# The first pair's down products directly behind its up products, the sort of all tokens after them

## The reference

```python
hid = jax.nn.silu(xi @ w1[e]) * (xi @ w3[e])
yb  = hid @ w2[e]                      # for the tokens that chose expert e
y   = y.at[buf_tok].add(yb * gate)     # two experts per token
```

## Time and profile before

| | |
|---|---|
| median of 3 runs | 2505.44 us |
| the profiled execution | 2509.44 us |
| its span | 2507.4 us |
| TensorE's matmuls busy | 2052.0 us (82%) |
| VectorE busy | 628.4 us (25%) |
| ScalarE busy | 417.3 us (17%) |
| DMA | 769.97 MB, mean 307 GB/s |

### The profile page before, as it was taken

The page is one execution under the profiler, slowest core; times in us unless marked ns, Lnnn a source line. Parts: engine busy times, 40 slices in busy tenths (PEclk is TensorE's granted clock), DMA queues, the critical chain, the costliest instruction groups (busy, mean ns, idle before and its releaser), DMA issues.

```text
span 2507.4 us, 29820 instructions
## 1 busy us (share of the span) xinstructions
PE 2052.0 (82%) x12400; PEld 1221.0 (49%) x12401; DVE 628.4 (25%) x1382; ACT 417.3 (17%) x780; POOL 0.2 (0%) x4
## 2 busy tenths in 40 slices
PE   7999996666667999756666799999877899999776
PEld 4775742222223684222222378885323678873333
DVE  2553330000012224000000244324211542244112
ACT  3141120000001212000000024212101233112111
POOL 0000000000000000000000000000000000000000
PEclk8999999999999999999999999999999999999999
DMA  9338759999999425999999942225999642257996
GB/s 402 126 142 374 319 232 426 426 426 426 426 426 427 171 93 219 425 426 426 426 426 426 425 182 106 97 107 224 426 425 426 258 164 101 101 202 294 425 426 279
DMA packets 66925, 769.97 MB, mean 307 GB/s; under 512 B 7424, under 2 KB 7936, under 8 KB 8448
## 3 DMA queue, kind: packets, MB, share of 16 engines
q1 hardware_dynamic: 66528, 768.19, 73.9%
q10 hardware_dynamic: 288, 0.26, 0.0%
HBM read 767.38 MB, written 1.05 MB: 306 GB/s over the span
## 4 chain that ended last, share of the span: by engine, by line
PE 53%; DMA 43%; DVE 2%; ACT 1%; issue 1%; SPq 0%; ACTq 0%; DVEq 0%
DMA slab<-in_triples 42%; PE psum L437 14%; PE psum L469 13%; PE psum L2107 5%; PE psum L734 5%; PE psum L2136 2%; PE psum L2032 2%; PE psum L540 2%; PE psum L2046 1%; DMA slab<-in_dense 1%; PE psum L2075 1%; PE psum L1284 1%; PE psum L2056 1%; PE psum L787 1%; DVE slab L677 0%
## 5 line engine op out<-in xcount | busy, mean ns | idle before, releaser
L2107 PE MATMUL psum<-slab 128*32 128x512 f32 (+1 forms) x3840 | 476.1, 599 | 329.4 <-DMA slab<-in_triples 327.4
L2107 PEld LDWEIGHTS psum<-slab 128*32 128x32 f32 x3840 | 160.6, 109 | 643.6 <-DMA slab<-in_triples 457.1
L437 PE MATMUL psum<-slab 128*128 128x256 f32 (+5 forms) x1464 | 372.2, 412 | 5.6 <-DVE slab L1885 3.8
L469 PE MATMUL psum<-slab 128*128 128x256 f32 x1504 | 340.2, 387 | 5.2 <-ACT slab L2345 2.3
L469 PEld LDWEIGHTS psum<-slab 128*128 128x128 f32 x1504 | 290.8, 194 | 53.1 <-issue 9.7
L437 PEld LDWEIGHTS psum<-slab 128*128 128x128 f32 (+2 forms) x1464 | 262.2, 190 | 107.6 <-issue 68.6
L2136 PE MATMUL psum<-slab 128*32 128x512 f32 (+1 forms) x1920 | 229.9, 604 | 52.4 <-DMA slab<-in_triples 52.4
L2191 DVE TENSOR_TENSOR slab<-psum,slab 128x512 f32<-128x512 f32 (+1 forms) x44 | 24.5, 558 | 783.5 <-PE psum L2107 546.0
L2032 PE MATMUL psum<-slab 128*128 128x256 f32 x704 | 171.5, 385 | 1.2 <-DVE slab L2195 1.2
L2032 PEld LDWEIGHTS psum<-slab 128*128 128x128 f32 x704 | 125.9, 189 | 52.0 <-issue 36.0
L2136 PEld LDWEIGHTS psum<-slab 128*32 128x32 f32 x1920 | 52.7, 110 | 177.6 <-issue 94.6
(11 more groups left out here) (461 smaller groups left out, 1453.7 us busy)
## 6 DMA issues: line engine op xcount, KB each, us to landing
slab<-in_triples SPq DMA_DIRECT2D x360, 1536.0 KB, 27.4
slab<-in_dense SPq DMA_DIRECT2D x73, 2048.0 KB, 10.3
slab<-in_pairs SPq DMA_DIRECT2D x18, 2048.0 KB, 8.4
slab<-in_dense SPq DMA_DIRECT2D x2, 1680.0 KB, 21.6
slab<-in_vec SPq DMA_DIRECT2D x1, 2589.5 KB, 32.9
slab<-in_dense SPq DMA_DIRECT2D x1, 1328.0 KB, 27.5
slab<-in_dense SPq DMA_DIRECT2D x2, 640.0 KB, 17.9
slab<-in_xT SPq DMA_DIRECT2D x1, 1024.0 KB, 8.7
```

The source lines that it names most:

```text
L437: ins = mm(out_ap, lhs, rhs, start=(n == 0), stop=(n == len(pairs) - 1), skip_group_check=True)
L469: ins = mm(psum[:, b, S * j:S * j + S], narrow(s, width)[:, k, c0 + P * j:c0 + P * j + P], src[:, k, :], start=(k == 0), stop=(k == KD - 1 ...
L2107: ins = mm(psum[WIN * g:WIN * g + WIN, n, :], xg[:, k, WIN * g:WIN * g + WIN], weights_of(w, j, g, extra), start=(k == 0), stop=(k == KD - ...
```

## The change

The sort moves behind the pair's down products, on all three engines. TensorE waits for both evictions of the down products before it, since the sort writes the same two banks; the first triple doesn't wait for them again. ScalarE's copies of the first triple's windows come after its part of the sort instead of before the eviction of the down products; VectorE turns the gates and evicts its half before its part of the sort.

```diff
@@ pe_pair
                 ins.then_inc(sems["unit_done"], 1)
-            pe_sort(q)
             fc = 4 if kind == 1 else 2
             pe_turn_hidden(q, fc)
...
                 ins.then_inc(sems["unit_done"], 1)
+            q.e.wait_ge(sems["half_ready"], q.due("half_ready"))
+            q.e.wait_ge(sems["results_ready"], q.due("results_ready"))
+            pe_sort(q)
@@ pe_triple
-            q.e.wait_ge(sems["half_ready"], q.due("half_ready"))
-            q.e.wait_ge(sems["results_ready"], q.due("results_ready"))
+            if not begin:
+                q.e.wait_ge(sems["half_ready"], q.due("half_ready"))
+                q.e.wait_ge(sems["results_ready"], q.due("results_ready"))
             pe_scatter(q, 0, KD // 2, begin)
@@ act_pass
-            if sort is not None:
-                act_sort(q, sort)
             q.e.wait_ge(sems["hid_turned"], q.due("hid_turned"))
             A.activation(hidT[:, 0:f // P, :], banks(0, 1, f // P, P), ACT.Copy).then_inc(sems["hidT_ready"], 1)
-            if ahead is not None:
+            if ahead is not None and sort is None:
                 act_windows(q, ahead)
             q.e.wait_ge(sems["unit_done"], q.due("unit_done", down))
             A.activation(ysl[:, 0:512], psum[:, 2, :], ACT.Copy).then_inc(sems["half_ready"], 1)
             q.skip("unit_done", 1 if pair or kind == 2 else 2)
+            if sort is not None:
+                act_sort(q, sort)
+                act_windows(q, ahead)
@@ dve_pair
             V.tensor_tensor(gated, gated, along(gates[:, :, 0:2], CAP), ALU.mult).then_inc(sems["gated_ready"], 1)
+            dve_gates_turned(q)
+            dve_results(q, 2)
             dve_sort(q, sort)
             dve_windows_copied(q, 0)
-            dve_gates_turned(q)
-            dve_results(q, 2)
```

## The result

The changed kernel took 2510.82 us, the median of 20 runs, against 2507.28 us for the kernel before, also of 20. The ratio is 1.0017 with a 95% interval of 1.0010 to 1.0023, so it is slower by 2.5 to 5.8 us. Measured again beside other kernels it was 1.0011 (1.0002 to 1.002). The forecast was 5.5 us slower, and 2510.9 us in time. That the time fits to 0.1 us is luck: the forecast started from 2505.4 us, the median of three runs, which is 1.8 us under the median of twenty, and its figure for the change is too high by about as much (5.5 us against 3.5 between the medians). The profiled execution has a span of 2509.2 us.

The account below looks back on a forecast made before the run. The stream of weight parts was taken to set each expert stage's time. At full clock 3.5 us faster, half clock 9.0 slower: net 5.5 slower, 2505.4 + 5.5 = 2510.9 us, range 2501.5 to 2518.

Parts of the forecast that it names:

- The chain of TensorE: Pair to first triple: new waits start the triple 3.9 us later in kind 1 (six slots), 6.45 in kind 2 (three).
- The stream at full clock: Weight parts per stage: gains of 2.8 and 2.5 us in kind 1, losses of 0.9 each in kind 2; 3.5 faster.
- Not removed but moved to the sort's other side: Kind 1 stream: the standstill from about 355 to 363 us would come from about 366 to 373 instead.
- The clock: TensorE's new gaps bring half clock: 1.3 us per kind 1 stage, 3.2 per kind 2 stage, 9.0 slower in all.
- A: TensorE's new gaps: no half clock follows them, so 3.5 us faster, 2501.9; chance 0.22.
- B: All four stages: half clock from before the first triple's first unit, 10.3 to 16 us slower, 2516 to 2521; chance 0.20.
- C: All stages: TensorE's lateness counts in full, 20.7 us, 2526; chance 0.03.
- D: Behind the sort: windows within 1 us and clock held, 2 us per stage more gained, 2494; chance 0.03.

Follow-up runs that it names:

- kernel with filled gaps: Changed kernel plus three idle matmul calls ahead of the transposes in kind 2 and three behind the sort in all four stages: 2504.24 us, 0.9982.
- the second profile: The changed kernel itself, unaltered, run again as reference beside the kernels with one fill: 2510.15 us, 1.0011.
- the fills one by one: Changed kernel plus three idle matmul calls in one place only: behind the sort in all stages 2507.59 us, ahead of kind 2's transposes 2506.80 us.
- each kind alone: Kernel before with the sort moved only in the two stages of one kind: kind 1 2502.69 us, kind 2 2516.36 us.
- hidden product first: Changed kernel with VectorE in kind 2 doing gates and hidden product before the windows' places: 2502.61 us, 0.9974.
- down inside: Kernel before with the pair's down products set between steps of the sort, into banks 4 and 5: 2490.56 us, 0.9931.
- fill ahead of the transposes: Changed kernel plus three idle matmul calls ahead of the hidden rows' transposes, in kind 2 only: 2506.80 us, 0.9997.
- the two probes: Kernel before plus four idle matmul calls per stage: behind the first triple's up products 2507.99 us, or behind the sort ahead of the pair's transposes 2521.41 us.
- kind 1 alone: Kernel before with the sort moved only in the two stages of kind 1 (six slots for the pair): 2502.69 us, 0.9975.

## Why the prediction was right

**The chain of TensorE.** Predicted waits and measured ones, kind 1: ahead of the transposes 0.97, measured 0.85; for the evictions 0.85, 0.84; for the windows 3.0, 3.25 and 2.82. Kind 2: 3.5, 3.40; 0.85, 0.84; 3.0, 2.82 and 3.00. Each was read from a row of the kernel before in which the same pair of instructions stood beside other work.

**The stream at full clock.** The kernel with filled gaps shows this term alone: gains of 2.5 and 2.6 us in kind 1 (predicted 2.8 and 2.5), losses of 0.7 and 1.0 in kind 2 (0.9 each), a net gain of 3.4 (3.5). "Not removed but moved to the sort's other side" is what the windows of the first stage show. In the third the standstill came a little later than forecast: counted from the pair's start, with 6.0 us added for its earlier start, it runs from 1754.6 to 1764.1 instead of 1753 to 1762, and the half clock's share is in its end.

**The clock.** Changed less filled, by stage: 0.9, 0.1, 2.7 and 3.3 us, 7.0 in all; in the second profile 0.6, 1.3, 3.0 and 3.3, 8.2. The forecast was 1.3 per stage of kind 1 and 3.2 per stage of kind 2, 9.0. By the medians the fills one by one give 6.0 for it. Ahead of kind 2's transposes it was priced at 2.0; the sort starts 12.0 us after up (1738.65 - 1719.54 - 7.09) where 9.5 was worked out at full clock, so TensorE is 2.5 late. In time this fill alone gave 3.4 / 2 = 1.7 per stage, and 2.3 where the gap behind the sort was filled already (0.9982 against 1.0000); 2.0 lies between them. Behind the sort it was priced at 1.2 in each stage; the fill alone gives 2.6 / 4, about 0.65, and 0.95 where the other gap was filled already (0.9982 against 0.9997). In the seven profiles with this gap unfilled (the changed kernel twice, each kind alone, hidden product first, down inside, fill ahead of the transposes) 18 of 24 gaps had the half clock behind them, and it began within or just ahead of the first unit, which restarts the stream (near 371.0 here, for a unit that began at 370.16). That unit took 2.0 us in the six others and 2.6 to 3.6 in the 18, 3.1 in the mean. So 1.1 us is lost where the clock falls, and 18/24 of it, 0.8 us, in the mean of all gaps. In the changed kernel's own trace the second and third stage had none, hence the 0.1 above. All eight gaps of 3.40, in kind 2, had it.

**The sum.** 5.5 us slower was forecast; 3.5 us between the medians, 2.5 to 5.8 by the interval. The term that was too large is the clock's share behind the sort, by 1 to 2 us over four stages: 1.2 was taken per gap, of which the traces show 0.8 and the times 0.65 to 0.95. The rest of the 2.0 us is within the noise.

**The rivals.** A (the clock holds) is the kernel with filled gaps: it was priced at 2501.9 and took 2504.24 beside a kernel before that was 2508.88 in that set, so -4.6 against -3.5; in the changed kernel itself the clock did not hold. B needed the half clock ahead of the first unit in all four stages; the two traces of the changed kernel have it there once in eight. C is ruled out by the two probes. D needed the windows within 1 us; they took 3.

Open: kind 1 alone gained 6.3 us (3.8 to 9.0) where its stages account for 3.1, and "hidden product first" 6.5 (4.0 to 9.3) where they account for 3.1 too. The trace of kind 1 alone is 7.4 us shorter than the one before, and 1.8 of that lies ahead of the first pair, where the two kernels are the same; so part may be scatter, but the medians of many executions keep the difference. Where the rest would be was not tried.

## What to carry to other kernels

Where a stream of transfers through a ring sets the time, ask of every move which release restarts the stream and how long the ring lasts until the next one: a move that frees one slot 14 us earlier and the next 4 us later mostly shifts the standstill (a gain of 2.5 us per stage at full clock). Look at what a long block hides, here a 3 us chain on VectorE and 3 us of copies, before it is moved: with the block cut and the short dependent steps put inside it the kernel gained 17 us, with the block behind them it lost 4. A gap of 3 us on TensorE can cost more than its length where what follows releases the stream, since half clock can follow; idle matmuls in it gave that part back, and another order on the engine that it waits for gave back most of the gap too.

## What the runs showed of the hardware

- Half clock behind a gap of 3.40 us, eight times of eight; behind 2.8 to 3.25 us, 18 times of 24. Behind the sort it cost 1.1 us in the unit that follows where it came, and 0.65 to 0.95 us of time in the mean of all gaps; ahead of the down products it made the sort about 2.5 us late (in one of the eight stages, with a shorter stretch at half clock, 1.4) and cost 1.7 to 2.3 us of time.
- The longest gap does not tell all: in the trace of the kernel before, a stretch at half clock (954.7 to 957.9) has no gap over 0.94 us in the 7 us ahead of it, and a gap of 2.45 us ahead of 239.35 had none behind it.
- Idle matmuls in a gap made the kernel faster although they compute nothing that is used: 2510.15 to 2506.80 us with six calls, three in each stage of kind 2.
- 3.7 us of added TensorE work cost nothing in one place of a stage and 3.2 us (12.8 / 4) some 20 us earlier.
